# Head norms of the second mixer: sums of squares through one block product, roots and inverses on whole tiles

## The reference, cut to what matters

```python
h = rms_norm_2(x, mix_norm[l])
(q_n, kc, vc, ksl, vsl, kwn, vwn, gts, q_s, k_s, v_s) = jnp.split(h @ w_in[l], split_at, axis=-1)

def rms_norm_2(x, g):
    return x * lax.rsqrt(jnp.mean(x * x, axis=-1, keepdims=True) + NORM_EPS) * g

q = apply_rope_2(rms_norm_2(q, g_q), ang)          # 8 heads of 64
ks = apply_rope_2(rms_norm_2(heads(k_sel), g_ks), ang)   # 2 heads of 64
kw = apply_rope_2(rms_norm_2(heads(k_win), g_kw), ang)   # 2 heads of 64
```

## Time and profile before

| | us |
|---|---|
| three runs | 2205.22, 2200.41, 2199.73 |
| median | 2200.41 |
| the profiled execution | 2201.26 |
| its span, first to last instruction | 2199.5 |

### The profile page before, as it was taken

How to read it: one execution, slowest core, us unless ns; L and a number is a source line. 1 busy time by engine, 2 the same in 40 slices (tenths; PEclk the granted TensorE clock), 3 DMA queues, 4 the chain that set the end, 5 groups by cost and what they waited for, 6 DMA issues and landing times.

```text
span 2199.5 us, 26529 instructions
## 1 busy us (share of the span) xinstructions
PE 2151.7 (98%) x11354; PEld 1760.3 (80%) x11354; DVE 1053.1 (48%) x1398; ACT 760.9 (35%) x1152; POOL 143.0 (7%) x103
## 2 busy tenths in 40 slices
PE   6999999999999999999999999999999999999999
PEld 4778778888888888888888888887877677888887
DVE  5758675555446333333543433364465356343322
ACT  5336442322235222223222222333456545222211
POOL 0064000000001000000111000000000002111000
PEclk9999999999999999999999999999999999999999
DMA  9421446556432333232333323323100022333232
GB/s 356 141 80 63 146 161 193 189 191 192 152 100 70 96 96 96 91 105 92 96 96 96 96 87 105 106 88 120 58 1 1 21 77 77 96 96 96 91 105 73
DMA packets 190901, 236.03 MB, mean 107 GB/s; under 512 B 4096, under 2 KB 175392, under 8 KB 190656
## 3 DMA queue, kind: packets, MB, share of 16 engines
q1 hardware_dynamic: 189696, 230.42, 32.6%
q0 software_dynamic: 1088, 3.92, 0.6%
HBM read 231.31 MB, written 2.10 MB: 106 GB/s over the span
## 4 chain that ended last, share of the span: by engine, by line
PE 88%; DVE 6%; ACT 3%; DMA 1%; issue 1%; SPq 0%; DVEq 0%; ACTq 0%
PE ps L473 25%; PE ps L475 25%; PE ps L474 25%; PE ps L749 3%; PE ps L679 2%; PE ps L784 1%; ACT pr L708 1%; PE ps L498 1%; DVE wl L382 1%; PE ps L569 1%; ACT wh L344 1%; DVE tmp L608 1%; DMA raw<-in_mix_out_w 1%; PE ps L2343 1%; PE ps L520 1%
## 5 line engine op out<-in xcount | busy, mean ns | idle before, releaser
L473 PE MATMUL ps<-xh,wh 128*128 128x512 f32 x1672 | 657.1, 393 | 3.6 <-DVE xT L799 1.3
L475 PE MATMUL ps<-xh,wl 128*128 128x512 f32 x1672 | 651.6, 390 | 0.0
L474 PE MATMUL ps<-xl,wh 128*128 128x512 f32 x1672 | 651.4, 390 | 0.0
L382 DVE TENSOR_TENSOR wl<-raw,wh 128x2048 fp32r<-128x2048 f32 (+2 forms) x168 | 374.5, 2229 | 471.4 <-ACT wh L344 471.3
L344 ACT CAST wh<-raw 128x2048 fp32r<-128x2048 f32 (+1 forms) x169 | 312.7, 1850 | 345.7 <-PE ps L475 262.0
L473 PEld LDWEIGHTS ps<-xh,wh 128*128 128x128 f32 x1672 | 313.6, 188 | 76.5 <-issue 7.4
L475 PEld LDWEIGHTS ps<-xh,wl 128*128 128x128 f32 x1672 | 313.5, 188 | 67.0
L474 PEld LDWEIGHTS ps<-xl,wh 128*128 128x128 f32 x1672 | 313.7, 188 | 66.2 <-issue 1.4
L474 PE MATMUL ps<-hl,wh 128*128 128x512 f32 x736 | 287.6, 391 | 0.0
L473 PE MATMUL ps<-hh,wh 128*128 128x512 f32 x704 | 274.1, 389 | 0.0
L475 PE MATMUL ps<-hh,wl 128*128 128x512 f32 x704 | 273.9, 389 | 0.0
(11 more groups left out here) (382 smaller groups left out, 2009.4 us busy)
## 6 DMA issues: line engine op xcount, KB each, us to landing
raw<-in_ffn_w SPq DMA_DIRECT2D x52, 1024.0 KB, 5.4
raw<-in_ada_w SPq DMA_DIRECT2D x40, 1024.0 KB, 5.4
raw<-in_ffn_wg SPq DMA_DIRECT2D x22, 1024.0 KB, 5.4
raw<-in_ffn_wu SPq DMA_DIRECT2D x22, 1024.0 KB, 5.4
raw<-in_ffn_w SPq DMA_DIRECT2D x16, 896.0 KB, 4.9
raw<-in_ffn_wd SPq DMA_DIRECT2D x16, 896.0 KB, 5.0
raw<-in_w_in SPq DMA_DIRECT2D x10, 1024.0 KB, 5.3
raw<-in_ffn_wd SPq DMA_DIRECT2D x8, 1024.0 KB, 5.1
```

What stands on the lines that cost most here:

```text
L382: e.tensor_tensor(wl[s][:, 0:n], r[:, 0:n], wh[s][:, 0:n].bitcast(F32), ALU.subtract).then_inc(*WLO.up(i))
L473: e.matmul(dst, ah, bh, start=start, stop=False)
L474: e.matmul(dst, ah, bl, start=False, stop=False)
L475: return e.matmul(dst, al, bh, start=False, stop=stop)
```

## The change

A new tile `eht` (128x512) is added. The sums of squares of q0 to q3, ks and kw are now one product with the constant `bd` on the stationary side, a 128x128 matrix with ones in two 64x64 blocks, and the squares as the 512 moving columns. Each channel row of the result then has the sum of its own head, so means, roots and inverses are taken on 128x512 and nothing is spread. The token term on all rows, `eht`, is ScalarE's square of the spread token roots times epsilon. The token roots are spread before they are inverted, and VectorE inverts them on 128x512. The new helpers:

```diff
+        def pe_head_totals(e, key, sq, bank):
+            e.wait_ge(*AF["square", key])
+            e.matmul(pb[bank], cst[:, CST["bd"]:CST["bd"] + P], tmp[sq][:, :], start=True, stop=True).then_inc(
+                *ST.up(("sums", key)))
+        def dve_head_totals(e, key, sq, bank):
+            e.wait_ge(*ST["sums", key])
+            e.scalar_tensor_tensor(out=tmp[sq][:, :], in0=pb[bank], scalar=1.0 / 64, in1=eht[:, :], op0=ALU.mult,
+                                   op1=ALU.add).then_inc(*VF.up(("mean", key)))
+        def act_head_totals(e, key, sq):
+            e.wait_ge(*VF["mean", key])
+            e.activation(tmp[sq][:, :], tmp[sq][:, :], ACT.Sqrt).then_inc(*AF.up(("root", key)))
+        def dve_head_factors(e, key, sq, src, gain):
+            e.wait_ge(*AF["root", key])
+            e.reciprocal(tmp[sq][:, :], tmp[sq][:, :]).then_inc(*VF.up(("inverse", key)))
+            e.wait_ge(*VF["inverse", key])
+            e.wait_ge(*AE["raw", key])
+            e.scalar_tensor_tensor(out=src, in0=src, scalar=gain, in1=tmp[sq][:, :], op0=ALU.mult, op1=ALU.mult).then_inc(
+                *VF.up(("normed", key)))
```

TensorE's list (`pe_w_in`):

```diff
-            pe_head_sums(e, "q0", 0, 8, VF["token term", 3])
-            pe_head_sums(e, "q1", 1, 16, VF["token term", 3])
             pe_proj(e, 3, u, P, xh, xl).then_inc(*MM.up(("in2", "q3"), ("w", u)))
-            e.wait_ge(*VF["inverse", 3])
+            e.wait_ge(*AF["root", 3])
             pe_spread(e, 3, 0, 1, T, 6)
-            pe_head_sums(e, "q2", 2, 24, VF["mean", "q1"])
...
             pe_proj(e, 0, u, 0, xh, xl).then_inc(*MM.up(("in2", "kc raw")))
-            pe_head_sums(e, "q3", 3, 32, VF["mean", "q2"])
-            e.wait_ge(*VF["roots in"])
-            pe_head_spread(e, "q0", 1, T, 6)
+            e.wait_ge(*AF["token terms"])
+            pe_head_totals(e, "q0", 0, 6)
             e.wait_ge(*AE["angles", 0])
-            pe_head_spread(e, "q1", 2, T, 4)
+            pe_head_totals(e, "q1", 1, 4)
...
-            pe_head_spread(e, "q2", 3, T, 5)
+            pe_head_totals(e, "q2", 2, 5)
             e.wait_ge(*AE["raw", "q2"])
-            pe_head_spread(e, "q3", 4, T, 2)
+            pe_head_totals(e, "q3", 3, 2)
...
-            pe_head_sums(e, "ks", 0, 8, VF["rotated", "q3"])
+            e.wait_ge(*VF["rotated", "q3"])
+            pe_head_totals(e, "ks", 0, 6)
...
-            pe_head_spread(e, "ks", 1, T, 6)
...
-            pe_head_sums(e, "kw", 1, 16, VF["mean", "ks"])
+            e.wait_ge(*VF["mean", "ks"])
+            pe_head_totals(e, "kw", 1, 6)
...
-            pe_head_spread(e, "kw", 2, T, 6)
```

ScalarE's list (`act_w_in`):

```diff
             act_head_in(e, "q2", 2, q2[:, 2, :], 2)
-            act_head_root(e, "q0", 1)
-            act_head_root(e, "q1", 2)
+            e.wait_ge(*VF["roots in"])
+            e.activation(eht[:, :], pb[6], ACT.Square, scale=float(np.sqrt(EPS))).then_inc(*AF.up("token terms"))
             act_head_in(e, "q3", 3, q2[:, 3, :], 3)
-            act_head_root(e, "q2", 3)
...
             act_ahead(e, of["q2", 2])
-            act_head_root(e, "q3", 4)
+            for c in range(4):
+                act_head_totals(e, f"q{c}", c)
             act_blocks(e, 0)
             act_ahead(e, of["ks"])
+            e.wait_ge(*VF["normed", "q0"])
             act_head_in(e, "ks", 0, ksT[:, 0, :], 0)
-            act_head_root(e, "ks", 1)
+            act_head_totals(e, "ks", 0)
...
+            e.wait_ge(*VF["normed", "q1"])
             act_head_in(e, "kw", 1, kwT[:, 0, :], 1)
             act_ahead(e, of["cmp", 0, 1])
-            act_head_root(e, "kw", 2)
+            act_head_totals(e, "kw", 1)
```

VectorE's list (`dve_w_in`), as it stands after the change up to vs, and the later lines that differ:

```diff
             e.wait_ge(*ST["spread", 3])
-            e.tensor_copy(rsm[:, :], pb[6]).then_inc(*VF.up("roots in"))
+            e.reciprocal(rsm[:, :], pb[6]).then_inc(*VF.up("roots in"))
+            e.reciprocal(rcol[:, :], hs[:, 0, 0:4]).then_inc(*VF.up("root columns"))
             dve_ahead(e, of["q2", 2])
             dve_compressed(e, 0, "kc raw")
+            dve_head_totals(e, "q0", 0, 6)
+            dve_head_totals(e, "q1", 1, 4)
             dve_blocks(e, 0)
+            for c in range(2):
+                dve_head_factors(e, f"q{c}", c, q2[:, c, :], gq)
             dve_compressed(e, 1, "vc raw")
+            dve_head_totals(e, "q2", 2, 5)
+            dve_head_totals(e, "q3", 3, 2)
+            for c in range(2, 4):
+                dve_head_factors(e, f"q{c}", c, q2[:, c, :], gq)
             dve_blocks_low(e, 0)
...
-            dve_head_mean(e, "ks", 1, 3)
-            dve_inverse(e, "ks", 1, 2, T)
+            dve_head_totals(e, "ks", 0, 6)
             dve_ahead(e, of["cmp", 0, 0])
-            dve_head_scaled(e, "ks", ksT[:, 0, :], v_("gks"), T)
+            dve_head_factors(e, "ks", 0, ksT[:, 0, :], v_("gks"))
...
-            dve_head_mean(e, "kw", 2, 3)
-            dve_inverse(e, "kw", 2, 2, T)
+            dve_head_totals(e, "kw", 1, 6)
...
-            dve_head_scaled(e, "kw", kwT[:, 0, :], v_("gkw"), T)
+            dve_head_factors(e, "kw", 1, kwT[:, 0, :], v_("gkw"))
```

More of the change, by code:

```diff
@@ L278, in program @@
         hidt = sb("hidt", [P, 256], F32, part)
+        eht = sb("eht", [P, T], F32, part)
         part.close()
@@ L2127, in dve_w_in @@
             dve_ahead(e, of["q2", 0])
[L2128 to L2131, removed]
             dve_ahead(e, of["q2", 1])
[L2133 to L2137, removed]
             e.wait_ge(*ST["spread", 3])
-            e.tensor_copy(rsm[:, :], pb[6]).then_inc(*VF.up("roots in"))
-            dve_head_mean(e, "q2", 3, 3)
-            dve_inverse(e, "q2", 3, 2, T)
+            e.reciprocal(rsm[:, :], pb[6]).then_inc(*VF.up("roots in"))
+            e.reciprocal(rcol[:, :], hs[:, 0, 0:4]).then_inc(*VF.up("root columns"))
             dve_ahead(e, of["q2", 2])
             dve_compressed(e, 0, "kc raw")
[L2144 to L2147, removed]
+            dve_head_totals(e, "q0", 0, 6)
+            dve_head_totals(e, "q1", 1, 4)
             dve_blocks(e, 0)
+            for c in range(2):
+                dve_head_factors(e, f"q{c}", c, q2[:, c, :], gq)
             dve_compressed(e, 1, "vc raw")
+            dve_head_totals(e, "q2", 2, 5)
+            dve_head_totals(e, "q3", 3, 2)
+            for c in range(2, 4):
+                dve_head_factors(e, f"q{c}", c, q2[:, c, :], gq)
             dve_blocks_low(e, 0)
-            dve_head_scaled(e, "q2", q2[:, 2, :], gq, T, 5)
-            dve_head_scaled(e, "q3", q2[:, 3, :], gq, T, 2)
             e.wait_ge(*AE["angles", 1])
@@ L2158, in dve_w_in @@
             dve_rope(e, "q3", 3, q2[:, 3, :], C2, S2, 0.125, bank=7)
-            dve_scaled(e, "vs", tmp[1][:, :], pb[2], rsm[:, :], ST["sums", "q1"])
-            dve_head_mean(e, "ks", 1, 3)
-            dve_inverse(e, "ks", 1, 2, T)
+            dve_scaled(e, "vs", tmp[1][:, :], pb[2], rsm[:, :], VF["normed", "q1"])
+            dve_head_totals(e, "ks", 0, 6)
             dve_ahead(e, of["cmp", 0, 0])
-            dve_head_scaled(e, "ks", ksT[:, 0, :], v_("gks"), T)
+            dve_head_factors(e, "ks", 0, ksT[:, 0, :], v_("gks"))
             dve_ahead(e, of["kw"])
@@ L2167, in dve_w_in @@
             dve_rope(e, "ks", 2, ksT[:, 0, :], C2, S2, 1.0)
-            dve_head_mean(e, "kw", 2, 3)
-            dve_inverse(e, "kw", 2, 2, T)
+            dve_head_totals(e, "kw", 1, 6)
             dve_blocks_low(e, 1)
             dve_ahead(e, of["vw"])
-            dve_scaled(e, "vw", tmp[0][:, :], pb[2], rsm[:, :], ST["sums", "ks"])
-            dve_head_scaled(e, "kw", kwT[:, 0, :], v_("gkw"), T)
-            dve_scaled(e, "gates", tmp[1][0:24, :], pb[0][0:24, :], rsm[0:24, :], ST["sums", "kw"])
+            dve_scaled(e, "vw", tmp[0][:, :], pb[2], rsm[:, :], VF["normed", "ks"])
+            dve_head_factors(e, "kw", 1, kwT[:, 0, :], v_("gkw"))
+            dve_scaled(e, "gates", tmp[1][0:24, :], pb[0][0:24, :], rsm[0:24, :], VF["normed", "kw"])
             dve_ahead(e, of["cmp", 1, 0])
```

## The result

The changed kernel takes 2209.05 us (median of 7 runs, 2207.35 to 2215.19) beside 2201.39 for the kernel before (7 runs, 2199.73 to 2205.22): ratio 1.0038, 95% interval 1.0029 to 1.0048, so 6.4 to 10.6 us slower.

A forecast was written before the change was run, and what follows sets the result against it. TensorE bounded the kernel; VectorE's seven inversions would become the bound in the head norms, delaying sq0 by 12.2 us despite TensorE's saving: 2201.26 + 12.2 = 2213.5, by the median 2212.6, stated 2213, range 2207 to 2220 (own range 2210 to 2216).

The forecast's parts named there:

- The inversion: On VectorE, seven RECIPROCAL passes on 128x512 standing in one row, each forecast at 3.4 us.
- R: Forecast time of one RECIPROCAL on 128x512 on VectorE: 3.4 us, with ends at 0.69 and 4.8.
- The rival of 8 to 9 ns a column: Steeper inversion on VectorE, 4.1 to 4.8 us each: +17 to +22 us, 2217 to 2222; chance 0.13.
- TensorE's saving: Head-norm sums and spreads replaced by six larger products: net -5.7 us, up to 7.3 with a clock dip gone.
- ScalarE held by `roots in`: ScalarE waits from 1421 for VectorE's token inversion, ending at 1429.6, with q3's copies and the ks cast queued behind.
- VectorE without gaps, TensorE waiting: From first mean to vs's scaling VectorE never pauses; TensorE waits 4.6 us for q0's rope, 3.3 at three later places.
- The clock as a rival: Low clock after each of TensorE's four pauses, 1.6 us each; all on the path +6.5 us, 2219; chance 0.05.
- the old dip: TensorE's clock at 0.56 for 3.70 us behind the small products with q2's sums; its 1.6 us loss may go.
- The sum: Walk through the head norms to the first stick-breaking product, sq0: start at 1507.3 instead of 1495.1, +12.2 us.
- plain-pass rival: Inversion costs 0.69 us: -3 to -4.7 us, 2196 to 2197; inversion under 2.6 us, shared with no change, chance 0.11.
- Kept to the end: Behind sq0 the old order holds and TensorE is the bound again, so the 12.2 us delay stays to the end.

The follow-up runs named there:

- the two sets: The changed kernel beside the kernel before, measured twice without a further edit: 2209.05 us, ratio 1.0038, then 2210.23 us, ratio 1.0044.
- plain passes: Changed kernel with all seven 128x512 inversions replaced by one plain pass each, so the result is no longer the network: 2193.14 us, 0.9967 of before.
- second trace: The changed kernel traced again with no edit, in more rounds beside the kernel before: 2210.23 us, ratio 1.0044.
- filling the first two: Changed kernel with 14, 10 and 11 unread products in TensorE's pauses before the ropes of q0, q1 and the ks totals: 2210.28 us, 1.0044 of before.
- batched: Ln and Exp kernel with the four query products moved ahead and four Ln, then four Exp, on ScalarE: 2196.60 us, 0.9979 of before.
- Ln and Exp in turns: Kernel with token terms taken before the token inversion, its six head factors formed by Ln and Exp on ScalarE: 2200.87 us, 0.9998 of before.
- tokens' terms first: Changed kernel with ScalarE squaring the token roots from PSUM before VectorE inverts them: 2207.57 us, 1.0038 of before.

## Why the prediction was right

The forecast was 2213 us by an inversion of 3.4 us on a row of VectorE without slack; 2209 to 2210 was measured, and the mechanism is the one described. The size was over-estimated: of the 12.2 us forecast 7.7 and 9.6 came in the two sets, and 2209.05 lies inside the stated 2207 to 2220 but under the narrower 2210 to 2216. By its steps, absolute times of after less the 0.3 us by which q0's copy is late there:

- **The inversion.** R = 3.35 us against 3.4. Of the slopes of the earlier trace rows the one between the two widest tiles was near: (3348 - 200) / 504 = 6.2 ns a column, against 6.0 from 4 to 8 columns. The rival of 8 to 9 ns a column falls. That 3.4 came so near is in part luck: a difference of 24 ns between small passes was carried to 64 times the width, and the slopes of the earlier trace rows allowed 3.2 to 4.8. By the repeat count of 8 of the Trainium skill's page "VectorE: DVE Perf Modes" (section "Walkthrough: the 8-slice pipeline in each mode") the estimate was 4.3 us; the trace has the direction of it and a lower price.
- **TensorE's saving.** It is there: with plain passes the stage is 5.7 us shorter. The prediction gave that rival 3 to 4.7; it took 2.8 us off for waits, and 1.6 were measured.
- **ScalarE held by `roots in`.** The 8.64 us wait names VectorE's inversions (the small one behind the large one). Freed of it, the stage is 1.6 to 1.9 us shorter.
- **VectorE without gaps, TensorE waiting.** Shown by the two timelines above. The pauses were forecast at 4.6, 3.3, 3.3 and 3.3 and are 3.85, 2.85, 0.81 and 3.09 (3.86, 1.91, none and 3.09 in the second trace). The third is short because TensorE ran at the low clock from 1450 to 1455, 5 x 0.47 = 2.4 us, which ate the pause.
- **The clock as a rival.** Dips followed the pauses, as the earlier trace rows had suggested, and were covered by the next wait, as the rival's counter-argument had it: filling the first two changed nothing, and the last cost 0 to 0.24 us. One step of the walk went otherwise for it: kw's product did not wait for its low part, which ended at 1474.72 + 1.23 = 1475.95; TensorE, at the low clock behind the totals of ks, came there 0.35 us later. VectorE's row did not wait for that product, so sq0 did not feel it. That the old dip goes with q2's small sums agrees with the row at 1430 to 1435, 1.00 after.
- **The sum.** +10.1 and +10.4 at sq0 against +12.2. The terms that were too large are small and many: a factor is 4.05 and not 4.2 (six of them, 0.9 us), a pair of means 1.2 and not 1.4. So the mean of ks ends 8.9 us late and not 10.3, kw's product starts 8.1 late and not 9.5, vw's 9.7 and not 11.4, sq0's 10.1. Some of the excess is in the additions: the steps named for kw's product make 1474.2 + 0.6 + 1.0 + 1.2 = 1477.0 and not 1477.4, those ahead of sq0's low part 1497.1 and not 1497.3, and compressed with two means stands as 2.2 where the same steps were 2.05 before. No row gives these 0.75 us. In the plain-pass rival 7.3 less 2.8 is 4.5, not 4.7.
- **Kept to the end.** 697.8 us behind sq0's pass against 698.1: nothing is recovered. The median difference of the first set, 7.7 us, is lower than the stage's, as are all medians of the table; the scatter ahead of the stage has this size, but that it is the reason is not shown.

## What to carry to other kernels

Moving per-token factors from 8 columns to full tiles trades many small TensorE products for wide elementwise passes. Price the dearest of these passes by its slope per column in the trace, and count how many of them stand in one row on an engine that others wait for. When such an operation goes to ScalarE, look at the table loads between its activations first: batched by function, in a list put in order for it, it was a gain of 5 us, in turns it was none.

## What was not expected of the hardware

- RECIPROCAL of 128x512 f32 takes 3348 ns from SBUF and 3356 ns from PSUM, 4.8 times the plain pass of 0.69 us; the source makes a difference of 8 ns.
- Ln and Exp in turns load a table each time, 1283 ns for a pass of 632 ns.
- In the memory attention, from 1585 to 1615 us, the clock was 1.00 throughout in three traces (plain passes, tokens' terms first, batched) and cost 1.7 to 5.1 us in the others, with the same instructions there. What decides between them was not tried.
